# Output projection begun inside a neighbourhood attention, and two expert blocks of three strips instead of four, in one program on one Trainium2 core

## The chip, the core and the metric

One core of one Trainium2 chip runs the whole program. The number that counts is the device time of one execution in microseconds (us); before the change it was 4483.69 us, the median of 3 runs (4479.28 to 4484.81). All data are float32. The engines are TensorE (PE, its weight loads PEld), VectorE (DVE), ScalarE (ACT), GpSimd (POOL) and SyncE (SP), which issues most of the DMAs.

## What is computed

Two blocks follow each other on one sequence of 1024 tokens with 1024 channels. The first block (two layers of linear attention) is untouched. The second has two layers; layer 0 mixes the tokens by neighbourhood attention, layer 1 by grouped-query attention, and both end in a mixture of 32 experts of which each token takes 2:

```python
for i in range(DEPTH):
    h = x * (1 + sc1) + sh1
    y = neighbourhood_mixer(h, ...) if i % 2 == 0 else gqa_mixer(h, ...)   # both end in "@ w_o"
    x = layer_norm_2(ALPHA * x + (1 + g1) * y, ...)
    h = x * (1 + sc2) + sh2
    y = hierarchical_moe(h, ...)
    x = layer_norm_2(ALPHA * x + (1 + g2) * y, ...)
# neighbourhood_mixer: qkv = h @ w_qkv; o = attention(q, k, v, rpb); return o.reshape(B, S, D) @ w_o
# hierarchical_moe:    (silu(xb @ w_gate[e]) * (xb @ w_up[e])) @ w_down[e], weighted by the gates
```

## The kernel before, in words

The program is a row of stages, each a block with one hand-written instruction list per engine and semaphores between them; at a stage's end all engines meet. Four stages matter here.

**The neighbourhood attention** (`neighbourhood_stage`, layer 0) goes over 8 pairs of heads, and in each over 8 token tiles of 128: 64 steps. A step i on PE is `scores(i + 1)` (L1659), three pieces of other work, `turn(i)` (transposes, L1672), again three or four pieces, `weigh(i)` (L1689). The other work is the projection of q, k and v for the next pair (`project`, L1632 and L1641), handed out by `advance(work, n)` from a generator, one matmul (or four small ones) at a time. The last pair (steps 56 to 63) has no next pair, so its generator is empty. A step's result goes to `mixT[:, pair, tokens]`: the pair is one of the 8 channel blocks over which the output projection sums. SP loads the output weights into `xT` as soon as the last projection has read it (L1620), long before the stage ends.

**The output projection and the routing** (`out_route_stage`, both layers) computes tile by tile `mixT^T W_o` (L2301: two halves of 512 columns, 8 channel blocks each, so 16 matmuls per tile), into banks 0 and 1 of PSUM for even tiles and 2 and 3 for odd ones. DVE takes the tile (L2378 to L2401: gate, residual, layer norm, scale and shift, `h_done`), PE turns h (L2283) and multiplies by the router's weights (L2292). PE's order is: tile 0, tile 1, turn(0), tile 2, turn(1), route(0), tile 3 and so on. The rows that DVE needs (gate, layer norm, scale, shift) are loaded by SP in the first microseconds of the stage (L1361). Then DVE works out the places of the tokens (a chain of small instructions, `skip_places` among them, called twice), and SP has meanwhile loaded the weights of the first expert and half of the second.

**The experts** (`experts_stage`, both layers) run 33 blocks in the order of a table (`TURNS`). Block b below 32 holds one expert; 0 and 1 are always experts 0 and 1 (so that their weights can be loaded early), the others are taken by their number of tokens, most first. Block 32 takes what one expert has too much. A block has 4, 3 or 2 strips of 32 rows; `strips_of` gives the number: 4 for blocks 0 to 7 and 32, 3 for 8 to 19, 2 for 20 to 31. The sum is 96 strips. What doesn't fit in an expert's block goes to an overflow block; more than one of them would start a loop of further blocks behind the stage. `blocks_in_turn` writes the table so that the strips stay near three per block. For a block of S strips PE does S times 32 matmuls for gate and up (`product`, L2593), transposes (L2580, L2604) and S times 16 matmuls for down (L2616); each matmul has two records in the profile. All weights stream from HBM: 4 MB for gate and up, 2 MB for down, each with two buffers. SP issues gate and up of block n+3 when the product of block n+1 is done (`up_ready`), and down of block n+2 when down of block n is done (`y_ready`):

```python
sp.wait_ge(up_ready, n + 2); load_gate_up(n + 3)
sp.wait_ge(y_ready, n + 1);  load_down(n + 2)
sp.wait_ge(y_copied, n + 1); store_rows(...)
```

**The clearing** (`clear_overflow`, L1529) writes zeros behind the rows of every block that has fewer than 128, in the background of the first block's last output stage.

## Time and profile before

| what | value |
|---|---|
| median of 3 runs | 4483.69 us |
| the profiled execution | 4486.34 us |
| its span in the profile | 4484.4 us |
| PE busy | 4098.7 us, 91% of the span |
| DVE, ACT, POOL busy | 2013.2, 1109.2, 509.0 us |
| mean granted PE clock | 0.958 of full |
| DMA moved | 710.31 MB, mean 158 GB/s |
| neighbourhood attention | 1705 to 2238 us of the span |
| output projection and routing, layer 0 | 2238 to 2420 us |
| experts, layer 0 and layer 1 | 2420 to 3009 us and 3832 to 4418 us |

The profile page gives shares over the whole span; the change touches four stages with different limits, so each is read by itself: its busy times by window, the order in time on PE, and who ended PE's waits. "Granted clock" is the share of full PE clock (2.4 GHz) that the chip allowed; 0.50 means 1.2 GHz.

### The profile page before, as it was taken

The page shows a single profiled execution, that of the slowest core. Times are in us where ns is not written, and L with a number is a line of the kernel's source. Part 1 is how long each engine was busy: PE and PEld are TensorE (multiplying, and loading weights), DVE is VectorE, ACT ScalarE, POOL GpSimd, SP SyncE. Part 2 cuts the span into 40 slices and gives each one's busy share as a digit, 9 for nine tenths or more (in the row PEclk, how much of TensorE's full clock was granted, in tenths as well). Part 3 has the DMA queues.
Part 4 walks back from the last instruction along what each step waited for, and adds up shares of the span by engine and source line. Part 5 has one row for each costly group of instructions (what it writes and reads, how often), then busy time and mean ns, then how long its engine had stood idle before and what let it go on. Part 6 is the DMA issues. An engine that isn't in the chain of part 4 may idle for free. (4 is left out here: it accounts for less than half of the span.)

```text
span 4484.4 us, 83646 instructions
## 1 busy us (share of the span) xinstructions
PE 4098.7 (91%) x36682; PEld 2459.4 (55%) x36682; DVE 2013.2 (45%) x2980; ACT 1109.2 (25%) x1919; POOL 509.0 (11%) x348
## 2 busy tenths in 40 slices
PE   7999999899999998999896999976999998899993
PEld 3555664445556645665454556543666664555652
DVE  4565356455545554555553111106657776111114
ACT  2333223134432221222200000003444530000003
POOL 1232011032211100000000000000312200000001
PEclk9999999999999999999897999987999998899996
DMA  3323202232320244445324999982000122799996
GB/s 103 113 95 104 61 24 90 72 109 90 109 82 28 85 160 84 76 79 90 78 82 170 394 393 401 403 327 80 15 2 14 39 82 85 265 399 400 403 395 257
DMA packets 285125, 710.31 MB, mean 158 GB/s; under 512 B 57307, under 2 KB 184739, under 8 KB 267735
## 3 DMA queue, kind: packets, MB, share of 16 engines
q1 hardware_dynamic: 271751, 658.70, 42.3%
q0 software_dynamic: 11808, 41.95, 2.8%
q8 instruction: 295, 4.83, 0.4%
q10 hardware_dynamic: 1200, 4.24, 0.2%
q14 instruction: 71, 0.58, 0.0%
HBM read 631.82 MB, written 64.60 MB: 155 GB/s over the span
## 5 line engine op out<-in xcount | busy, mean ns | idle before, releaser
L493 PE MATMUL ps<-sb_xT,sb_work 128*128 128x512 f32 x768 | 359.9, 605 | 9.6 <-ACT sb_x_tok L846 5.5
L493 PE MATMUL ps<-sb_mixT,sb_work 128*128 128x512 f32 x768 | 359.5, 604 | 9.6 <-ACT sb_x_tok L846 5.5
L1632 PE MATMUL ps<-sb_xT,sb_work 128*128 128x512 f32 x512 | 236.2, 600 | 0.0
L2593 PE MATMUL ps<-sb_work,sb_mixT 128*32 128x256 f32 x3584 | 208.7, 388 | 12.4 <-DMA sb_work<-moe_w_up 11.7
L493 PEld LDWEIGHTS ps<-sb_xT,sb_work 128*128 128x128 f32 x768 | 138.0, 192 | 148.1 <-issue 130.1
L493 PEld LDWEIGHTS ps<-sb_mixT,sb_work 128*128 128x128 f32 x768 | 138.0, 192 | 147.8 <-issue 129.9
L2593 PE MATMUL ps<-sb_work,sb_xT 128*32 128x256 f32 x3584 | 204.9, 383 | 6.7 <-DMA sb_work<-moe_w_up 5.9
L2108 DVE TENSOR_REDUCE sb_cols<-ps 128x1 f32<-128x1024 f32 x128 | 150.6, 1218 | 85.8 <-PE ps L1951 85.7
L2677 DVE TENSOR_TENSOR sb_work<-ps,sb_work 128x512 f32<-128x512 f32 (+2 forms) x66 | 61.6, 933 | 260.2 <-PE ps L2616 260.2
L2660 ACT COPY sb_work<-ps 128x256 f32<-128x256 f32 (+2 forms) x66 | 31.0, 470 | 591.6 <-PE ps L2604 591.6
L2593 PEld LDWEIGHTS ps<-sb_work,sb_mixT 128*32 128x32 f32 x3584 | 117.1, 112 | 92.0 <-issue 22.7
L2593 PEld LDWEIGHTS ps<-sb_work,sb_xT 128*32 128x32 f32 x3584 | 116.0, 111 | 83.5 <-issue 14.3
L2593 PE MATMUL ps<-sb_mixT,sb_xT 128*32 128x256 f32 x2560 | 151.2, 390 | 11.0 <-DMA sb_mixT<-moe_w_up 10.0
L1927 PE MATMUL ps<-sb_work,sb_mixT 128*128 128x384 f32 x448 | 154.4, 491 | 3.2 <-PEq L93 3.2
L2593 PE MATMUL ps<-sb_xT,sb_mixT 128*32 128x256 f32 x2560 | 147.7, 383 | 8.9 <-DMA sb_xT<-moe_w_up 8.0
L2683 DVE TENSOR_TENSOR sb_work<-sb_work,ps 128x256 f32<-128x256 f32 (+2 forms) x66 | 35.8, 542 | 263.9 <-ACT sb_work L2650 263.9
L1632 PEld LDWEIGHTS ps<-sb_xT,sb_work 128*128 128x128 f32 x512 | 91.1, 190 | 104.2 <-issue 104.2
L2032 ACT ACTIVATE sb_work<-ps,sb_cols 128x1024 f32<-128x1024 f32 x128 | 142.7, 1115 | 17.9 <-DVE sb_cols L2108 12.3
L1961 PEld LDWEIGHTS ps<-sb_const,sb_work 128*128 128x128 f32 x1024 | 109.7, 141 | 63.1 <-issue 32.7
L2616 PE MATMUL ps<-sb_work 128*32 128x256 f32 x2560 | 144.1, 379 | 0.0
L1961 PE MATMUL ps<-sb_const,sb_work 128*128 128x128 f32 x1024 | 141.0, 280 | 1.9 <-DVE sb_work L2116 0.9
L1951 PE MATMUL ps<-sb_work 64*128 64x512 f32 x512 | 130.6, 629 | 6.7 <-ACT sb_work L2032 3.7
(486 smaller groups left out, 7268.4 us busy)
## 6 DMA issues: line engine op xcount, KB each, us to landing
sb_work<-moe_w_gate SPq DMA_DIRECT2D x34, 2048.0 KB, 8.2
sb_work<-moe_w_up SPq DMA_DIRECT2D x34, 2048.0 KB, 12.6
sb_work<-moe_w_down SPq DMA_DIRECT2D x32, 2048.0 KB, 21.3
sb_mixT<-moe_w_down SPq DMA_DIRECT2D x17, 2048.0 KB, 22.2
sb_xT<-moe_w_down SPq DMA_DIRECT2D x17, 2048.0 KB, 22.0
sb_xT<-moe_w_gate SPq DMA_DIRECT2D x16, 2048.0 KB, 16.0
sb_xT<-moe_w_up SPq DMA_DIRECT2D x16, 2048.0 KB, 22.1
sb_mixT<-moe_w_gate SPq DMA_DIRECT2D x16, 2048.0 KB, 15.9
```

Source lines behind the costliest of these rows:

```text
L493: last = pe.matmul(m.ps[:, bank, :], b.w[i][:, k, :], m.xT[:, k, half * HALF:(half + 1) * HALF], start=(k == 0), stop=(k == NK - 1))
L1632: last = pe.matmul(m.ps[:, bank, :], w[j // 2][:, k, :], m.xT[:, k, j % 2 * HALF:(j % 2 + 1) * HALF], start=(k == 0), stop=(k == NK - 1))
L1927: last = pe.matmul(m.ps[:, bank, 0:WIDE], m.xT[:, k, n * P:(n + 1) * P], w[:, k, :], start=(k == 0), stop=(k == NK - 1))
L1951: last = pe.matmul(m.ps[:, 2 * head + half, :], q[g % 2][j][d, t * P:(t + 1) * P], k2[g % 2][d, half * HALF:(half + 1) * HALF], start=True ...
L1961: last = pe.transpose(m.ps[:, 4 + half, b * P:(b + 1) * P], prob[i % 2][head][:, half * HALF + b * P:half * HALF + (b + 1) * P], ident(m))
L2032: act.activation(prob[i % 2][head], banks(m, 2 * head), ACT.Exp, bias=top[:, column(i, head)], accum_out=total[:, column(i, head)]).then_i ...
L2108: dve.tensor_reduce(top[:, column(i, head)], banks(m, 2 * head), AX.X, ALU.max, negate=True).then_inc(found, 1)
L2593: last = pe.matmul(strip_sums(2 + 2 * (n % 2), tile[j])[:, g, :], b.x_turned[n % 2][:, k, g * STRIP:(g + 1) * STRIP], b.gate_up[n % 2][:, ...
L2616: last = pe.matmul(strip_sums(6, tile[j])[:, g, :], b.act_turned[n % 2][:, g, tile[k]], b.down[n % 2][:, k, j * 2 * P:(j + 1) * 2 * P], st ...
L2660: act.copy(b.act_turned[n % 2][:, 0:strips[n], :], chunks(m.ps[:, 0, :])[:, 0:strips[n], :]).then_inc(h_copied, 1)
L2677: dve.tensor_tensor(b.y[n % 2][:, 0:strips[n], :], strip_sums(6)[:, 0:strips[n], :], each_chunk(b.gate_row, strips[n]), ALU.mult).then_inc ...
L2683: dve.tensor_tensor(act, act, strip_sums(2 + 2 * (n % 2))[:, 0:strips[n], P:2 * P], ALU.mult).then_inc(multiplied, 1)
```

## The change

Three things are edited.

1. In the last pair of the neighbourhood attention, from its fourth tile (step 59) on, PE gets pieces to do: the output projection of three half tiles, over the 7 channel blocks that are finished then. `OUT_BEGUN` names (tile, half, bank): (0, 0, 6), (0, 1, 7), (1, 0, 2), so 21 matmuls. Two pieces stand before `turn` and three after it. Ahead of the first PE waits for the output weights. The output stage of layer 0 then computes only the eighth channel block of these three half tiles; tile 0 lies in banks 6 and 7 there, not 0 and 1. Layer 1 gets `begun=()` and stays as it was.
2. Blocks 0 and 1 have 3 strips instead of 4, in both layers: 94 strips. The table of turns is made anew with that start. Counted with the reference's own routing on its inputs, experts 0 and 1 get 81 and 55 tokens in layer 0, and 54 and 68 in layer 1; three strips hold 96.
3. `skip_places` has one more DVE instruction (it must know the narrower first blocks), and the clearing writes two more places of 32 rows.

```diff
-    places = [(b, rows_of(b)) for b in range(WIDE_BLOCKS, N_EXPERTS)] + [(b, 0) for b in range(N_FIXED, N_BLOCKS)]
+    places = [(b, rows_of(b)) for b in range(N_EXPERTS) if rows_of(b) < P] + [(b, 0) for b in range(N_FIXED, N_BLOCKS)]
...
+OUT_BEGUN = ((0, 0, 6), (0, 1, 7), (1, 0, 2))
...
+            def begin_out():
+
+                pe.wait_ge(out_loaded, 16 * (NK // 2))
+                for t, half, bank in OUT_BEGUN:
+                    for k in range(pairs - 1):
+                        pe.matmul(m.ps[:, bank, :], m.mixT[:, k, t * P:(t + 1) * P], m.xT[:, k, half * HALF:(half + 1) * HALF],
+                                  start=(k == 0), stop=False)
+                        yield
...
-                    work = project(pair + 1) if pair + 1 < pairs else iter(())
+                    work = project(pair + 1) if pair + 1 < pairs else begin_out()
                 if i + 1 < count:
                     scores(i + 1)
-                advance(work, 3)
+                if pair + 1 < pairs or t >= 3:
+                    advance(work, 3 if pair + 1 < pairs else 2)
                 turn(i)
-                advance(work, 3 if t < NT - 1 else 4)
+                if pair + 1 < pairs or t >= 3:
+                    advance(work, 3 if t < NT - 1 else 4)
                 weigh(i)
...
-    return 4 - (block >= WIDE_BLOCKS) - (block >= MIDDLE_BLOCKS) if block < N_EXPERTS else 4
+    if block >= N_EXPERTS:
+        return 4
+    return 4 - (block < N_FIRST) - (block >= WIDE_BLOCKS) - (block >= MIDDLE_BLOCKS)
...
-    order, strips = list(range(N_FIRST)), 4 * N_FIRST
+    order, strips = list(range(N_FIRST)), 3 * N_FIRST
...
+    def y_bank(t):
+        return 6 if t == 0 and begun else 2 * (t % 2)
...
-                    for k in range(NK):
-                        last = pe.matmul(m.ps[:, 2 * (t % 2) + half, :], m.mixT[:, k, t * P:(t + 1) * P],
+                    for k in range(NK - 1 if (t, half, y_bank(t) + half) in begun else 0, NK):
+                        last = pe.matmul(m.ps[:, y_bank(t) + half, :], m.mixT[:, k, t * P:(t + 1) * P],
...
-                do(dve.tensor_scalar(spare, at, MIDDLE_BLOCKS - 0.5, None, ALU.is_gt))
+                do(dve.tensor_scalar(spare, at, N_FIRST - 0.5, None, ALU.is_lt))
+                do(dve.scalar_tensor_tensor(spare, at, MIDDLE_BLOCKS - 0.5, spare, ALU.is_gt, ALU.add))
```

How the instructions stand now at the places that matter. PE from the scores of step 63 to the second tile of layer 0's output projection (L1659 scores, L1672 turn, L1689 weigh, L2301 projection, L2283 turning h), before:

```order
L1659 MATMUL ps<-sb_work 128x384 x2
L1672 MATMUL ps<-sb_const,sb_work 128x128 x6
L1689 MATMUL ps<-sb_work 64x128 x6
L1672 MATMUL ps<-sb_const,sb_work 128x128 x6
L1689 MATMUL ps<-sb_work 64x128 x6
L1573 UNCONDITIONAL_BRANCH
L2275 UNCONDITIONAL_BRANCH
L2301 MATMUL ps<-sb_xT,sb_mixT 128x512 x32
L2283 MATMUL ps<-sb_const,sb_work 128x128 x8
L2301 MATMUL ps<-sb_xT,sb_mixT 128x512 x16
```

The same place with the change (L1661, L1674, L1691, L2320 and L2302 are the same lines moved down, L1700 the new pieces):

```order
L1661 MATMUL ps<-sb_work 128x384 x2
L1700 MATMUL ps<-sb_xT,sb_mixT 128x512 x2
L1674 MATMUL ps<-sb_const,sb_work 128x128 x6
L1700 MATMUL ps<-sb_xT,sb_mixT 128x512 x3
L1691 MATMUL ps<-sb_work 64x128 x6
L1700 MATMUL ps<-sb_xT,sb_mixT 128x512
L1674 MATMUL ps<-sb_const,sb_work 128x128 x6
L1691 MATMUL ps<-sb_work 64x128 x6
L1575 UNCONDITIONAL_BRANCH
L2294 UNCONDITIONAL_BRANCH
L2320 MATMUL ps<-sb_xT,sb_mixT 128x512 x11
L2302 MATMUL ps<-sb_const,sb_work 128x128 x8
```

Steps 59 to 62 have five new matmuls each, step 63 has one, and the first two tiles of the output stage have 11 matmuls left of 32.

PE in the first blocks of the experts, before:

```order
L2593 MATMUL ps<-sb_work,sb_mixT 32x256 x128
L2580 MATMUL ps<-sb_const,sb_mixT 128x128 x8
L2593 MATMUL ps<-sb_xT,sb_mixT 32x256 x32
L2604 MATMUL ps<-sb_const,sb_work 128x128 x4
L2593 MATMUL ps<-sb_xT,sb_mixT 32x256 x32
L2580 MATMUL ps<-sb_const,sb_mixT 128x64 x8
L2593 MATMUL ps<-sb_xT,sb_mixT 32x256 x64
L2616 MATMUL ps<-sb_mixT,sb_work 32x256 x64
```

With the change (L2613, L2600, L2624, L2636 are the same lines moved down):

```order
L2613 MATMUL ps<-sb_work,sb_mixT 32x256 x96
L2600 MATMUL ps<-sb_const,sb_mixT 128x96 x8
L2613 MATMUL ps<-sb_xT,sb_mixT 32x256 x32
L2624 MATMUL ps<-sb_const,sb_work 128x128 x3
L2613 MATMUL ps<-sb_xT,sb_mixT 32x256 x32
L2600 MATMUL ps<-sb_const,sb_mixT 128x96 x8
L2613 MATMUL ps<-sb_xT,sb_mixT 32x256 x32
L2636 MATMUL ps<-sb_mixT,sb_work 32x256 x48
```

The products of blocks 0 and 1 have 96 matmuls each instead of 128. The strips by turn were 4, 4, 2, 2, twelve times 3, then six times (4, 2), then 4, 2, 2, 2, 2; now they are fourteen times 3, then six times (4, 2), then 4 and six times 2. So the stage ends with six narrow blocks in place of four.

## Rows read from the trace of the kernel before

**Rows 1.** Windows of the last pair; columns: us, busy (x count) by engine, PEclk, DMA
```profile
2188.00:2238.00 50.00, 28.70 (x172) 17.69 (x172) 27.21 (x77) 12.15 (x36) 0.00 (x0) 0.73 0.21 85
2200.00:2204.00 4.00, 4.00 (x22) 2.44 (x18) 1.34 (x5) 0.57 (x2) 0.00 (x0) 0.50 0.02 5
...
2238.00:2242.00 4.00, 3.79 (x5) 1.65 (x6) 0.67 (x7) 1.28 (x1) 0.13 (x1) 0.57 0.68 240
```

**Rows 2.** Timeline of PE: start, us, line, shapes, count, idle time before
```profile
2172.55 0.92 PE L1659 MATMUL ps<-sb_work 64*128 64x384 f32 x4
...
2180.23 0.92 PE L1659 MATMUL ps<-sb_work 64*128 64x384 f32 x4
...
2210.22 1.65 PE L1659 MATMUL ps<-sb_work 64*128 64x384 f32 x4
...
2233.45 0.88 PE L1689 MATMUL ps<-sb_work 128*64 128x128 f32 x12 [1.71 <-ACT sb_work L1745]
...
2238.21 29.40 PE L2301 MATMUL ps<-sb_xT,sb_mixT 128*128 128x512 f32 x64 [1.50 <-PEq L93]
2267.45 1.04 PE L2283 MATMUL ps<-sb_const,sb_work 128*128 128x128 f32 x8
2268.32 13.90 PE L2301 MATMUL ps<-sb_xT,sb_mixT 128*128 128x512 f32 x32
```

**Rows 3.** Timeline of DVE in layer 0's output projection, first tile
```profile
2241.76 0.69 DVE L2366 TENSOR_SCALAR sb_work<-sb_work 128x1024 f32<-128x1024 f32 x1 [3.04 <-DMA sb_work<-scratch_mods]
2253.99 1.23 DVE L2378 TENSOR_TENSOR sb_work<-ps,sb_work 128x1024 f32<-128x1024 f32 x1 [11.53 <-PE ps L2301]
...
2258.07 1.28 DVE L2391 SCALAR_TENSOR_TENSOR sb_x_tok<-sb_x_tok,sb_moments,sb_work 128x1024 f32<-128x1024 f32 x1
...
2261.97 1.22 DVE L2401 TENSOR_TENSOR sb_work<-sb_work 128x1024 f32<-128x1024 f32 x1
```

**Rows 4.** Timeline of SP, the last row loads; then landing times of line L1361
```profile
2239.51 1.22 SPq L1361 DMA_DIRECT2D sb_work<-scratch_mods  x2
...
DMA to landing us min/median/max: 3.4/6.1/9.3
```

**Rows 5.** Timeline of DVE, start of `skip_places`
```profile
2394.00 0.18 DVE L2457 TENSOR_SCALAR sb_work<-sb_work 128x32 f32<-128x32 f32 x1
2394.22 0.19 DVE L2458 SCALAR_TENSOR_TENSOR sb_work<-sb_work 128x32 f32<-128x32 f32 x1
```

**Rows 6.** SP's own waits in the stage with the clearing: total, times, longest
```profile
SPq L1384 <- PEq L1384: 28.9, 1, 28.9
```

**Rows 7.** Windows of the experts of layer 0, same columns as rows 1
```profile
2457.00:2700.00 243.00, 234.08 (x3981) 141.44 (x3973) 28.12 (x41) 18.68 (x40) 11.79 (x13) 0.99 1.02 393
...
2900.00:2950.00 50.00, 47.47 (x798) 28.51 (x794) 5.52 (x8) 3.98 (x8) 1.79 (x2) 0.97 0.98 379
```

**Rows 8.** Timeline of SP: gate of the third and of the fourth block
```profile
2439.42 0.40 SPq L2724 DMA_DIRECT2D sb_work<-moe_w_gate  x1
...
2457.08 0.34 SPq L2724 DMA_DIRECT2D sb_xT<-moe_w_gate  x1
```

**Rows 9.** Timeline of PE in the experts: two unhindered middle blocks
```profile
2529.39 3.64 PE L2593 MATMUL ps<-sb_work,sb_mixT 128*32 128x256 f32 x64
...
2541.56 5.36 PE L2616 MATMUL ps<-sb_work 128*32 128x256 f32 x96
2546.74 3.64 PE L2593 MATMUL ps<-sb_xT,sb_mixT 128*32 128x256 f32 x64
```

**Rows 10.** Timeline of PE: blocks that waited for gate and up
```profile
2510.32 5.35 PE L2593 MATMUL ps<-sb_xT,sb_mixT 128*32 128x256 f32 x64 [3.84 <-DMA sb_xT<-moe_w_up]
...
2656.53 3.66 PE L2593 MATMUL ps<-sb_xT,sb_mixT 128*32 128x256 f32 x64 [2.31 <-DMA sb_xT<-moe_w_up]
...
2923.36 5.35 PE L2593 MATMUL ps<-sb_work,sb_mixT 128*32 128x256 f32 x64 [2.53 <-DMA sb_work<-moe_w_up]
...
2990.88 6.26 PE L2593 MATMUL ps<-sb_work,sb_mixT 128*32 128x256 f32 x64 [4.93 <-DMA sb_work<-moe_w_up]
```

More of the change, by code:

```diff
@@ L1550, in neighbourhood_stage @@
     bias_loaded, moved, masked = (s["loaded_d"], s["loaded_e"]), s["prefetched"], s["signal_0"]
+    out_loaded = s["stored"]
     (projected, evicted, scored, biased, exponent, inverted, normalised, turned_a, turned_b, copied_a, copied_b,
@@ L1617, in _ @@
                     load_weights(2, pair + 1)
-            load_out_weights(sp, m, a["na_w_o_2"][0], s["stored"])
-            sp.wait_ge(s["stored"], 16 * (NK // 2))
+            load_out_weights(sp, m, a["na_w_o_2"][0], out_loaded)
+            sp.wait_ge(out_loaded, 16 * (NK // 2))
         @block.tensor
@@ L2200, with out_route_stage @@
 TURNS = blocks_in_turn()
-def out_route_stage(nc, m, l, a, ln_g, ln_b, gate, modulate, x_affine=None):
+def out_route_stage(nc, m, l, a, ln_g, ln_b, gate, modulate, x_affine=None, begun=()):
     s = m.sem
@@ L2377, in _ @@
                 dve.wait_ge(y_ready, t + 1)
-                dve.tensor_tensor(y[t % 2], banks(m, 2 * (t % 2)), gate_row, ALU.mult).then_inc(y_gated, 1)
+                dve.tensor_tensor(y[t % 2], banks(m, y_bank(t)), gate_row, ALU.mult).then_inc(y_gated, 1)
                 dve.wait_ge(y_gated, t + 1)
@@ L3009, in program @@
         x_affine = (a["ln_g_2"][l - 1, 1], a["ln_b_2"][l - 1, 1]) if l else None
-        out_route_stage(nc, m, l, a, a["ln_g_2"][l, 0], a["ln_b_2"][l, 0], mods[l][2], mods[l][3:5], x_affine)
+        out_route_stage(nc, m, l, a, a["ln_g_2"][l, 0], a["ln_b_2"][l, 0], mods[l][2], mods[l][3:5], x_affine,
+                        begun=OUT_BEGUN if l % 2 == 0 else ())
         ln_rows = a["ln_g_2"][l, 1], a["ln_b_2"][l, 1]
```

## The prediction

> **What bounds the kernel now.** I read the windows first, then PE's timeline, then the waits, each for the stages that the change touches. In the last pair of the neighbourhood attention PE is busy 28.70 of 50 us [rows 1]: the pair has no projection to mix in, so each step is a chain from scores over DVE and ScalarE to the weighted sum. PE stands between the links, and the granted clock falls to 0.50, which is 1.2 GHz, even while PE is busy all of 4 us. The same 4 us show a DMA share of 0.02: the output weights, which SP fetches before, have landed by about 2200, ten microseconds before the first new matmul may ask for them at 2210.22. In the output projection PE has no gap (64 records in 29.40 us, then 32 in 13.90 us) and DVE waits 11.53 us for it [rows 2, 3]: PE bounds it. In the experts both PE and the DMA engines are full: DMA share 1.02 at 393 GB/s over 243 us [rows 7]. Who ends the waits decides it. From turn 5 (2510.32) to turn 32 (2990.88) PE began a block every 17.80 us, and waited for gate and up at both ends and between [rows 10]; an unhindered block of three strips takes PE 2546.74 - 2529.39 = 17.35 us [rows 9]. So the stream of weights sets the pace, by a narrow margin.
>
> **The change part by part.** All steps are against the profiled execution (4486.34 us, which is 2.65 us above the median of the runs).
>
> *The moved matmuls, where they go.* A 128x512 matmul takes PE 13.90 / 16 = 0.87 us at full clock [rows 2]. A step of a full pair, with six of them, takes 2180.23 - 2172.55 = 7.68 us [rows 2]; with five it is 7.68 - 0.87 = 6.8. That is longer than the chain of a last-pair step at full clock, so PE sets the step. Step 59's part begins with the scores at 2210.22 at the low clock (1.65 us against 0.92) [rows 2]. PE then has work without a gap, and at 2238 the full clock came back within about 4 us (0.57 over the first 4), at a price of 29.40 - 2 x 13.90 = 1.6 us [rows 1, 2]. I take that price once: step 59 is 6.8 + 1.6 = 8.4, three further steps are 20.4, so the sum of step 62 (`weigh`) ends at 2239.0 and begins at 2238.2 instead of 2233.45. Step 63 has one matmul, 0.87. The stage ends **5.6 us later** (4.8 + 0.87). Bounds: 3 us, if the clock is back sooner and the old idle time of 1.7 us before each `weigh` hides a part; 10 us, if it is back a step and a half later.
>
> *Where they come from.* The first two tiles keep 11 of 32 matmuls: 11 x 0.87 = 9.6 us. But turn(0) needs DVE's first tile. From the stage's start s = 2238.21, DVE's gate row is ready at s + 4.2 (2241.76 + 0.69) [rows 3]. From there the part up to the moments takes 2258.07 - 2253.99 = 4.1 us, to s + 8.3 [rows 3]. Then DVE needs the scale and shift rows: the last are issued from 2239.51 for 1.22 us and land up to 9.3 us later, about 2249.7, s + 11.4 [rows 4]. The remaining part takes 2261.97 + 1.22 - 2258.07 = 5.1, so h is done at s + 16.5. Before, turn(0) began at 2267.45 = s + 29.2 [rows 2]. The gain is **12.7 us**, not the 18.3 of 21 matmuls: PE is out of work at s + 9.6 and stands some 7 us for the row loads. That is a new wait, and turn(0) and tile 2 are queued behind it. It is long enough for the clock: after the last pair's gaps the row shows 0.50 [rows 1], so I charge the 1.6 us again. From tile 2 on PE is the bound again, since DVE needs about 10 us per tile and PE 16. The Trainium skill (TensorE: Matmul & The Clock Gate, the section on the HAM clock gate) says that the throttled clock is the default and only sustained activity lifts it; by that rule the new gap costs the clock, as charged; with a clock that ignored gaps the sum would be 1.6 us better. Net of this part: 5.6 - 12.7 + 1.6 = **-5.5 us**. Bounds -9 and 0.
>
> *The experts.* A strip costs PE 3.6 us in the product and 5.36 / 3 = 1.8 in down [rows 9]. Two strips fewer would be 10.8 us of PE, but PE is not the pace. What the edit does to the stream: SP issued gate and up of turn 2 at 2439.42 when product 0 was done, and of turn 3 at 2457.08 when product 1 was done [rows 8]. Between, 4 MB at 393 GB/s [rows 7] take 10.7 of 17.7 us, so the engines ran dry; only from the second issue on is the stream whole. That issue now comes after two products of three strips, 2 x 3.6 = 7.2 us earlier. Thereafter the same 30 pairs of matrices go through. The strips save 128 KB each in the two stores and one gather behind that point, 0.39 MB or 1.0 us. The stream stays whole: a block moves 6.3 MB of weights and 0.8 MB of tokens and results, 7.1 MB or 18 us at 393 GB/s, and the fourteen blocks of three strips ask for the next load every 17.35 us. The wide blocks may leave a hole, as now (0.98 in one window [rows 7]); I take off 0.7. The end is unchanged: the last block has two strips in both. So **-7.5 us per layer**, -15.0 for both (the second runs the same program). Bounds per layer: -8.5, and -1 (rival B).
>
> *Small edits.* `skip_places` has one instruction more, called twice per layer, on DVE's chain to the experts: 2394.22 - 2394.00 = 0.22 us [rows 5], four times, **+0.9 us**. The two added clearing writes of 128 KB each cost nothing: SP stood 28.9 us at the end of that stage waiting for PE alone [rows 6]; without this cover they would cost under 2 us.
>
> Sum: -5.5 - 15.0 + 0.9 = **-19.6 us**: 4466.7 against the profiled execution, 4464.1 against the median.
>
> **The rivals.**
>
> B, *PE is the pace of the experts and the narrow tail eats the gain.* For it: between the waits of rows 10 most blocks ran without one, and 17.35 is only 3% below 17.80. Then the shorter products save 10.8 us of PE, but the stage now ends in six narrow blocks instead of four. PE needs 17.35 - 5.4 = 12.0 us for one, the stream (2990.88 - 2923.36) / 4 = 16.9 [rows 10], so two more blocks wait 4.9 each: -10.8 + 9.8 = -1.0 per layer. Total -5.5 + 0.9 - 2.0 = -6.6: 4477.1. Against it: PE waited 4.93 us for the last block and the DMA share is 1.02. The Trainium skill (DMA: Bandwidth & Descriptors, "Where 436 GB/s comes from") gives the fabric 435 GB/s and HBM 358 per core; at the first a block of 7.1 MB would take 16.3 us, below PE's 17.35, and B would hold; the trace has 393 and 379 [rows 7], between the two, and decides against it. Chance 0.15.
>
> C, *the low clock stays* (the slower side). If the full clock isn't granted from step 59 to the end of tile 2, a step takes 2 x 2.4 for its own work and 5 x 1.74: 13.5 us. Four steps and step 63 end the stage 31 us later; the first two tiles take 19.1 instead of waiting until 16.5, so the gain falls to 10.1; tile 2 costs 13.9 more. 31 - 10.1 + 13.9 + 0.9 - 15 = +20.7: 4504.4. Each us of low clock costs half a us, so it decides from some 60 us of low clock on. For it: 0.50 with PE fully busy [rows 1]. Against: at 2238 it was gone after a few us of gapless work [rows 2]. Chance 0.04.
>
> D, *the projection gives nothing*: the stage ends 10 us later (the clock comes back late) and the output stage gains 10 to 11. Total -14: 4469.7. Chance 0.10.
>
> E, *the change doesn't do what it says*: experts 0 or 1 have over 96 tokens, a second overflow block starts the loop behind the stage. One more block of 6.3 MB at 393 GB/s with nothing beside it, 16 us, then some 23 of PE for four strips: +39 per layer, 4503 or more. The counts in the description (at most 81) exclude it but for a slip. Chance 0.01.
>
> **How the numbers follow.** A measurement of this kernel can tell about 0.2%, 9.0 us. My forecast has 0.70, its own range is 4457 to 4471. It and D lie beyond 9 us; of B a third does, if the tail eats less. Faster 0.70 + 0.10 + 0.05 = 0.85; within 0.2%: 0.10 of B and 0.01 of C, 0.11; slower 0.03 + 0.01 = 0.04. The range for 8 in 10 runs from 4456 (both bounds on the good side) to 4477 (B).
>
> **What would show it.** Right: from step 59 on a step of about 6.8 us at clock 1.00; an idle time of 6 to 7 us on PE before the first turn of h, with DVE's first tile ending 16 to 17 us after the stage's start; gate and up of turn 3 issued some 7 us earlier after the stage's start; waits for gate and up of about 5 us at most of the last five turns; an experts stage shorter by 7 to 8 us in both layers. Wrong: the experts' stage shorter by 1 to 3 us with DMA share under 1.00 in the middle (B); clock 0.50 beyond the first two new matmuls (C, D); a gap on PE of under 3 us in the output stage, which would say that the rows land earlier than I take them to and that more than 12.7 us is gained.

## The result and the profile after

| | before | after |
|---|---|---|
| median, runs of one call | 4481.48 us (4 runs, 4474.98 to 4484.81) | 4454.57 us (4 runs, 4447.35 to 4456.38) |
| ratio, 95% interval | | 0.9934 [0.9922, 0.9946] |
| the profiled execution, its span | 4486.34, 4484.4 us | 4455.61, 4453.7 us |
| PE busy, records | 4098.7 us | 4066.9 us, x36294 (388 fewer) |
| DMA moved | 710.31 MB | 709.73 MB |

Forecast was 4464.1 in a range of 4456 to 4477. The kernel became 27 us faster instead of 19.6, and its median lies 1.4 us below the range's low end. Between the two profiled executions the difference is 30.7 us:

| stretch | before | after | difference | forecast |
|---|---|---|---|---|
| start of the attention | 1709.09 | 1707.83 | -1.3 | not touched |
| attention, to the start of the output stage | 529.12 | 535.27 | +6.15 | +5.6 |
| from there to the first turn of h | 29.24 | 17.00 | -12.24 | -12.7 |
| first to second turn of h | 14.60 | 16.81 | +2.21 | +1.6 |
| second turn of h to the first expert product | 140.51 | 140.59 | +0.1 | +0.45 |
| experts, layer 0 (first product to last matmul's end) | 586.51 | 574.49 | -12.0 | -7.5 |
| experts, layer 1 | 583.26 | 570.83 | -12.4 | -7.5 |
| between and behind the experts | 892.07 | 890.88 | -1.2 | +0.45 |

The forecast column has the prediction's term for each stretch. The attention and the output stage came out 1.6 us worse than forecast in sum (-3.9 against -5.5), the experts gained 9.4 us more. The 1.3 us ahead of the attention lie within the scatter: its start lies between 1706.0 and 1709.7 us in all the traces here. PE around the new matmuls, timeline of after (columns as in [rows 2]):

```profile
2208.98 1.65 PE L1661 MATMUL ps<-sb_work 64*128 64x384 f32 x4
2210.56 3.33 PE L1700 MATMUL ps<-sb_xT,sb_mixT 128*128 128x512 f32 x4
...
2217.86 0.92 PE L1661 MATMUL ps<-sb_work 64*128 64x384 f32 x4
...
2224.65 0.92 PE L1661 MATMUL ps<-sb_work 64*128 64x384 f32 x4
...
2243.10 9.68 PE L2320 MATMUL ps<-sb_xT,sb_mixT 128*128 128x512 f32 x22 [1.50 <-PEq L93]
2260.10 1.97 PE L2302 MATMUL ps<-sb_const,sb_work 128*128 128x128 f32 x8 [7.32 <-DVE sb_work L2420]
2261.86 15.21 PE L2320 MATMUL ps<-sb_xT,sb_mixT 128*128 128x512 f32 x32
2276.91 1.04 PE L2302 MATMUL ps<-sb_const,sb_work 128*128 128x128 f32 x8
```

Step 59 takes 2217.86 - 2208.98 = 8.88 us (forecast 8.4), the next 6.79 (6.8). Then the new wait: PE stands 7.32 us ahead of the first turn of h, and behind it the low clock, 1.97 us for a turn that takes 1.04 and 15.21 for a tile that takes 13.90 [rows 2]. That is 0.93 + 1.31 = 2.2 us. What PE waited for stands on DVE, first tile (timeline of after; [rows 3] before):

```profile
2246.62 0.69 DVE L2385 TENSOR_SCALAR sb_work<-sb_work 128x1024 f32<-128x1024 f32 x1 [3.00 <-DMA sb_work<-scratch_mods]
...
2251.19 0.21 DVE L2405 BATCH_NORM_AGGREGATE sb_moments<-sb_stats 128x2 f32<-128x12 f32 x1
2254.92 1.28 DVE L2410 SCALAR_TENSOR_TENSOR sb_x_tok<-sb_x_tok,sb_moments,sb_work 128x1024 f32<-128x1024 f32 x1 [3.52 <-DMA sb_work<-scratch_mods]
...
2258.82 1.22 DVE L2420 TENSOR_TENSOR sb_work<-sb_work 128x1024 f32<-128x1024 f32 x1
```

DVE waits twice, for the gate row and for scale and shift, which land 11.8 us after the stage's start at 2243.10 (forecast 11.4). PE no longer holds DVE: the 11.53 us of [rows 3] are gone.

In the experts, SP's issues of the third and fourth block's gate (after; [rows 8] before):

```profile
2431.10 0.40 SPq L2744 DMA_DIRECT2D sb_work<-moe_w_gate  x1
...
2444.88 0.34 SPq L2744 DMA_DIRECT2D sb_xT<-moe_w_gate  x1
```

From the first product (2417.50, before 2422.56) to the second of these issues it is 27.38 us, before 34.52: 7.1 us earlier, in layer 1 7.5. Forecast was 7.2. PE in that stage (timeline of after; [rows 9, 10] before):

```profile
2466.69 3.64 PE L2613 MATMUL ps<-sb_xT,sb_mixT 128*32 128x256 f32 x64
...
2484.04 3.64 PE L2613 MATMUL ps<-sb_work,sb_mixT 128*32 128x256 f32 x64
...
2501.39 3.64 PE L2613 MATMUL ps<-sb_xT,sb_mixT 128*32 128x256 f32 x64
...
2623.45 3.66 PE L2613 MATMUL ps<-sb_work,sb_mixT 128*32 128x256 f32 x64 [0.40 <-DMA sb_work<-moe_w_up]
...
2925.77 5.77 PE L2613 MATMUL ps<-sb_xT,sb_mixT 128*32 128x256 f32 x64 [6.06 <-DMA sb_xT<-moe_w_up]
...
2943.74 5.32 PE L2613 MATMUL ps<-sb_work,sb_mixT 128*32 128x256 f32 x64 [3.63 <-DMA sb_work<-moe_w_up]
...
2959.54 3.66 PE L2613 MATMUL ps<-sb_xT,sb_mixT 128*32 128x256 f32 x64 [1.90 <-DMA sb_xT<-moe_w_up]
...
2975.01 5.05 PE L2613 MATMUL ps<-sb_work,sb_mixT 128*32 128x256 f32 x64 [3.24 <-DMA sb_work<-moe_w_up]
```

Blocks follow each other every 17.35 us, and in layer 0 the first wait for weights comes 206 us after the first product (0.40 us at 2623.45). Before, turn 5 waited 3.84 us, 88 us after the first product [rows 10]. The sum of these waits in layer 0 hardly changed, 19.7 to 19.0 us; most of it now stands in the tail, behind the wide blocks.

The part that was not forecast is the stream. I call stream the time from the issue of the fourth block's gate to the first matmul that uses the last block's up: 533.80 and 532.71 us before (layers 0 and 1), 530.13 and 527.50 after, so 3.7 and 5.2 us shorter, where the forecast had 0.3. Windows of 60 us, the first and the third behind that issue (columns: us, busy (x count) of PE, PEld, DVE, ACT, POOL, PEclk, DMA share, GB/s), after:

```profile
2444.88:2504.88 60.00, 59.98 (x1045) 36.06 (x1037) 7.54 (x11) 4.36 (x9) 2.72 (x3) 1.00 1.02 396
2564.88:2624.88 60.00, 59.60 (x1041) 35.79 (x1036) 7.72 (x11) 4.85 (x10) 2.77 (x3) 1.00 1.02 399
```

and before:

```profile
2457.08:2517.08 60.00, 56.16 (x939) 33.65 (x935) 7.36 (x11) 4.21 (x10) 2.71 (x3) 0.97 1.00 381
2577.08:2637.08 60.00, 57.24 (x992) 34.41 (x985) 7.52 (x11) 4.34 (x9) 2.71 (x3) 1.00 1.02 384
```

Between the two lies one window of 402 GB/s in both. In the 180 us the new kernel moves (15 + 0 + 15) GB/s x 60 us = 1.8 MB more, which is 4.5 us of stream. From then on the rates agree: 399 GB/s to the end of the stream, 400 before. A part of the first window belongs to the start and not to what follows: its DMA share is 1.00 before and 1.02 after, and over all complete kernels with loads asked for as in these two it is 0.98 to 1.00 where blocks 0 and 1 have four strips, 1.02 where they have three.

### The profile page after: what moved, and what is told of

The parts are those of the page before. It is cut to its first block and busy times, and to the rows that moved or that the text cites. A ratio compares the mean times of both kernels' runs of the same rounds, so it can differ in the third digit from the quotient of the medians.

```text
span 4453.7 us, 82876 instructions
## 1 busy us (share of the span) xinstructions
PE 4066.9 (91%) x36294; PEld 2439.0 (55%) x36294; DVE 2011.5 (45%) x2984; ACT 1109.3 (25%) x1919; POOL 509.4 (11%) x348
## 2 busy tenths in 40 slices
DMA packets 284642, 709.73 MB, mean 159 GB/s; under 512 B 57339, under 2 KB 184259, under 8 KB 267255
## 5 line engine op out<-in xcount | busy, mean ns | idle before, releaser
L2613 PE MATMUL ps<-sb_work,sb_mixT 128*32 128x256 f32 x3520 | 204.3, 387 | 10.7 <-DMA sb_work<-moe_w_up 10.0
L2613 PE MATMUL ps<-sb_work,sb_xT 128*32 128x256 f32 x3520 | 202.7, 385 | 8.8 <-DMA sb_work<-moe_w_up 8.1
L2680 ACT COPY sb_work<-ps 128x384 f32<-128x384 f32 (+2 forms) x66 | 30.6, 464 | 581.3 <-PE ps L2624 581.3
L2697 DVE TENSOR_TENSOR sb_work<-ps,sb_work 128x768 f32<-128x768 f32 (+2 forms) x66 | 60.6, 918 | 254.2 <-PE ps L2636 254.2
L2613 PEld LDWEIGHTS ps<-sb_work,sb_mixT 128*32 128x32 f32 x3520 | 114.4, 112 | 88.5 <-issue 21.0
L2613 PEld LDWEIGHTS ps<-sb_work,sb_xT 128*32 128x32 f32 x3520 | 114.0, 111 | 85.1 <-issue 17.2
L2613 PE MATMUL ps<-sb_xT,sb_mixT 128*32 128x256 f32 x2496 | 144.6, 384 | 9.6 <-DMA sb_xT<-moe_w_up 9.0
L2613 PE MATMUL ps<-sb_mixT,sb_xT 128*32 128x256 f32 x2496 | 145.6, 386 | 8.4 <-DMA sb_mixT<-moe_w_up 7.8
L2703 DVE TENSOR_TENSOR sb_work<-sb_work,ps 128x384 f32<-128x384 f32 (+2 forms) x66 | 35.3, 535 | 247.1 <-ACT sb_work L2670 247.1
L2636 PE MATMUL ps<-sb_work 128*32 128x256 f32 x2496 | 140.6, 379 | 0.0
L1741 ACT ACTIVATE sb_work<-sb_work,sb_cols 128x384 f32<-128x384 f32 x128 | 77.6, 607 | 238.2 <-DVE sb_cols L1786 238.2
```

What stands on the lines that cost most here:

```text
L1741: act.activation(p, p, ACT.Exp, bias=top[:, column(i, head)], scale=-1.0, accum_out=total[:, column(i, head)]).then_inc(exponent, 1)
L2613: last = pe.matmul(strip_sums(2 + 2 * (n % 2), tile[j])[:, g, :], b.x_turned[n % 2][:, k, g * STRIP:(g + 1) * STRIP], b.gate_up[n % 2][:, ...
L2636: last = pe.matmul(strip_sums(6, tile[j])[:, g, :], b.act_turned[n % 2][:, g, tile[k]], b.down[n % 2][:, k, j * 2 * P:(j + 1) * 2 * P], st ...
L2680: act.copy(b.act_turned[n % 2][:, 0:strips[n], :], chunks(m.ps[:, 0, :])[:, 0:strips[n], :]).then_inc(h_copied, 1)
L2697: dve.tensor_tensor(b.y[n % 2][:, 0:strips[n], :], strip_sums(6)[:, 0:strips[n], :], each_chunk(b.gate_row, strips[n]), ALU.mult).then_inc ...
L2703: dve.tensor_tensor(act, act, strip_sums(2 + 2 * (n % 2))[:, 0:strips[n], P:2 * P], ALU.mult).then_inc(multiplied, 1)
```

## The experiments

### Splitting the change

What was to be told apart: how much each half gives, and whether the surplus in the experts comes from the two narrower blocks (an earlier issue) or from the new order of the turns.

**Projection alone:** the change, with blocks, order and `skip_places` of before.

```diff
-    return 4 - (block < N_FIRST) - (block >= WIDE_BLOCKS) - (block >= MIDDLE_BLOCKS)
+    return 4 - (block >= WIDE_BLOCKS) - (block >= MIDDLE_BLOCKS)
...
-    order, strips = list(range(N_FIRST)), 3 * N_FIRST
+    order, strips = list(range(N_FIRST)), 4 * N_FIRST
```

> Only the begun output projection; the experts as in the kernel before. My forecast of this part was -5.5 us; the trace of the change reads 4.9 us later at the end of the attention, 12.2 us gained up to the first turn of h, 2.2 us lost to the low clock behind the gap: -5.1 in sum. If the traces tell the truth: 4 to 6 us faster than before. If the extra gain of the whole change lies in this part (a second effect of the fillers): 10 us or more faster.

Measured: 4481.77 us against 4482.77, ratio 0.9996 [0.9987, 1.0005], 11 runs. By the time alone no gain can be told; the interval reaches from -5.8 to +2.2 us. Its trace shows the stretches of after to a tenth of a microsecond: attention 535.31, first turn of h at 16.96, from the attention's start to the first expert product 709.66 us against 709.67 after and 713.47 before. So this half gives 3.8 us. That stretch repeats well: it is 713.5 to 713.7 us in the four traces without the moved matmuls and 709.3 to 709.7 in the eight with all 21 of them. The expert stages, which the edit leaves as before, hide it in the total: in this trace they are 588.3 and 584.6 us against 586.5 and 583.3, together 3.2 us longer.

**Experts alone:** `begun=()`, no pieces in the last pair.

```diff
-                    work = project(pair + 1) if pair + 1 < pairs else begin_out()
+                    work = project(pair + 1) if pair + 1 < pairs else iter(())
```

> Only the two narrower first blocks with the new order of turns and the longer skip_places; no projection begun. My forecast of this part was -15.0 + 0.9 = -14.1 us. The two traces read -12.0 and -12.4 us for the two experts stages. If that is real and not a difference between two single executions: 23 us faster than before. If it is scatter: 14 us.

Measured: 4458.16 us, ratio 0.9945 [0.9932, 0.9959], -24.6 us. The forecast of this half was -14.1, or -23 if the traces of the stages were right. Nearly the whole gain is the experts'. The two halves add up: -1.0 and -24.6 give -25.6, the change measured -26.9.

**Strips alone:** as "experts alone", with the order of turns of before.

```diff
-TURNS = blocks_in_turn()
+TURNS = [0, 1, 20, 21, 8, 9, 10, 11, 12, 13, 14, 15, 16, 17, 18, 19, 32, 22, 2, 23, 3, 24, 4, 25, 5, 26, 6, 27, 7, 28, 29, 30, 31]
```

> As e2, but the turns in the order of before: strips 3, 3, 2, 2, twelve times 3 and so on, four narrow blocks at the end. Theory S (the stream of weights sets the pace all through; only its start matters): the start is 7.2 us earlier as in e2, so the same time as e2. Theory P (PE's own work sets the pace in most of the stage and the order decides how much of it is lost in waits): slower than e2 by 4 us or more in both layers together, because turns 2 and 3 are narrow, PE runs ahead early and waits at turn 5 as in the kernel before (3.8 and 4.1 us).

Measured: 4462.79 us, ratio 0.9953 [0.9939, 0.9967], -20.0 us. The fourth block's gate is issued 7.5 and 8.3 us earlier, the streams are 534.1 and 531.5 us, as before. Its stages end 576.8 and 575.4 us after the first product. The early waits are back, 60 and 79 us behind the first product (PE, timeline of this kernel):

```profile
2482.05 3.66 PE L2611 MATMUL ps<-sb_work,sb_mixT 128*32 128x256 f32 x64 [2.36 <-DMA sb_work<-moe_w_up]
...
2501.62 4.93 PE L2611 MATMUL ps<-sb_xT,sb_mixT 128*32 128x256 f32 x64 [3.85 <-DMA sb_xT<-moe_w_up]
```

Against "experts alone" the old order costs 4.6 us (4462.79 against 4458.16, the fastest execution of the one just behind the slowest of the other). But the -20.0 are 5.9 us more than the forecast of -14.1, which had no term for the order; against the trace of before its two stages are only some 17.5 us shorter. Where the rest comes from is open.

**Order alone:** before, with the planner started at six strips, so the new order stands with blocks 0 and 1 still of four.

```diff
-    order, strips = list(range(N_FIRST)), 4 * N_FIRST
+    order, strips = list(range(N_FIRST)), 3 * N_FIRST
```

> The kernel before with only the order of turns of the change: blocks 0 and 1 keep 4 strips, then twelve times 3, and six narrow blocks at the end. Theory S: no issue of the stream moves, 0 +- 2 us against before. Theory P: the early wait at turn 5 goes, 4 to 8 us faster in both layers together, unless the longer narrow tail takes it back.

Measured: 4475.86 us, ratio 0.9983 [0.9974, 0.9992], -6.9 us, 11 runs. No early waits: the first stands 392 us behind the first product. Streams 532.3 and 529.9 us. The first and the third window of its stream:

```profile
2454.87:2514.87 60.00, 60.00 (x1050) 36.11 (x1046) 7.35 (x10) 4.45 (x9) 2.72 (x3) 1.00 0.99 372
2574.87:2634.87 60.00, 60.00 (x1039) 36.23 (x1042) 7.32 (x11) 5.31 (x11) 3.66 (x4) 1.00 1.02 402
```

and the third of "strips alone":

```profile
2569.37:2629.37 60.00, 56.20 (x965) 34.04 (x955) 6.87 (x10) 4.34 (x9) 2.74 (x3) 1.00 1.02 381
```

So both edits gain: the strips by the earlier issue, the order by a shorter stream. The order's part is what the forecast left out.

### Is it PE or the stream?

**Less PE:** from the third turn on the products sum over 5 of 8 channel slices; the loads stay.

```diff
-            for k in range(NK):
+            for k in (range(NK) if n < 2 or n_blocks == 1 else (*range(NK // 2), NK - 1)):
```

> The change, but the products of all turns from the third on sum over 5 of their 8 slices of channels (3 are left out), so PE has about 4 us less per block and the stream alone sets the pace. Only layer 0 is read, since the wrong values route layer 1 otherwise. The stream is the time from the issue of turn 3's gate to the first matmul of turn 32; in the change 530.1 us, with the old order 533 to 537. Theory S (the stream is whole and its rate is the chip's): 528 to 532 as before, with PE waiting in nearly every turn. Theory P (PE's work held the stream back): 520 or less, rate above 405 GB/s. Theory L (the stream runs slower when PE is behind it and waits, as in the old order between 120 and 180 us after turn 3's issue, 384 GB/s against 399 to 406): 535 or more, at 390 GB/s.

Its values differ from then on, so layer 1 routes its tokens otherwise, and layer 0 is the one to read. Measured once: 4460.82 us. The stages end 575.5 and 575.1 us after the first product (after: 574.5, 570.8), the streams are 533.4 and 532.6. PE is busy for 77 us less in the stream of layer 0 (434.6 against 511.1, though at a mean clock of 0.91 instead of 0.99) and the stage is no shorter. The stream lies between what the expectation gave to S (528 to 532) and to L (535 or more), so neither is met. Totals of PE's waits (us in total, times, longest) in layer 0, this kernel:

```profile
PE ps L2613 <- DMA sb_work<-moe_w_up: 52.3, 15, 6.6
PE ps L2613 <- DMA sb_xT<-moe_w_up: 46.5, 14, 6.4
```

and after:

```profile
PE ps L2613 <- DMA sb_work<-moe_w_up: 10.0, 5, 3.6
PE ps L2613 <- DMA sb_xT<-moe_w_up: 9.0, 3, 6.1
```

What PE saves comes back as waits: 98.8 us against 19.0. Rival B had PE as the pace, and falls here. The surprise is in the windows (same columns; the first, third and fifth behind the issue of the fourth block's gate):

```profile
2446.75:2506.75 60.00, 54.01 (x844) 31.18 (x840) 7.53 (x11) 4.83 (x10) 2.71 (x3) 0.91 1.02 384
2566.75:2626.75 60.00, 45.82 (x717) 26.46 (x709) 6.32 (x10) 4.34 (x9) 2.76 (x3) 0.94 1.02 389
...
2686.75:2746.75 60.00, 50.85 (x776) 29.36 (x772) 6.91 (x10) 4.92 (x11) 3.69 (x4) 0.91 1.02 412
```

At the same DMA share of 1.02 the engines move 384 to 389 GB/s where PE waits from the start, against 396 to 402 where it doesn't. Yet in the fifth window it is 412, and PE still waits there: it does so at 29 of the 33 blocks of this stage. And the first window of "order alone" has 372 GB/s at a share of 0.99 with a PE that never waits. So whether PE waits does not decide the rate by itself. The Trainium skill (DMA: Bandwidth & Descriptors, "Where 436 GB/s comes from") gives 358 GB/s for HBM per core; this stream is above it in every window of before, after and "less PE", so no ceiling at that figure is seen here.

**Less PE, old order:** the same edit with the table of "strips alone".

> As e9, with the turns in the order of before and blocks 0 and 1 of three strips. Theories S, P and L: the same stream as e9 within 2 us, because the order mattered only through PE. If the order itself sets the rate of the stream (which sizes of stores and gathers stand beside which loads), it is again 3 to 5 us longer than e9.

Measured once: 4461.93 us, streams 534.2 and 535.0, 384 GB/s over the first 180 us of the stream (387 in "less PE"). With PE out of the way the two orders lie 0.8 us apart in layer 0, the layer to read, and 2.4 in layer 1. Single executions with one and the same order differ by up to 4.0 us in layer 0 (528.3 to 532.3), so this fits an order that works through the time at which PE is done with its blocks, but it does not show it: an effect of a few us on the transfers themselves would not be seen in one run each.

**Half of down:** the reverse, half of each down matrix not loaded from the third turn on.

```diff
-                sp.dma_start(b.down[n % 2], source(n, "down").rearrange("(k p) n -> p k n", p=P)).then_inc(loads[n % 2][1], 16)
+                k = slice(0, QUARTERS) if n < 2 else slice(0, QUARTERS // 2)
+                sp.dma_start(b.down[n % 2][:, k, :], source(n, "down").rearrange("(k p) n -> p k n", p=P)[:, k, :]).then_inc(
+                    loads[n % 2][1], 16)
```

> The change, but from the third turn on only the first half of each down matrix is loaded (1 MB less per block, 6.0 instead of 7.05 MB), PE's work as it was. Only layer 0 is read. PE is then the pace: no waits for gate and up, and the stage lasts as long as PE's own work, that is its 570.8 us less the 18.9 us of waits and about 4 us of low clock behind them: 547 to 549 us. If it stays above 555, something other than the bytes of the stream (the issue behind up_ready, the latency) makes PE wait.

Measured once: 4422.75 us; both stages end 555.0 and 555.1 us after the first product. I had expected 547 to 549, but counted from the 570.8 us at which the last group of matmuls in after begins, not ends; counted so, this stage takes 551.4 us. What is left of the miss, 2 to 4 us, is about the 4 us of low clock that I had taken off. The window over the stream of layer 0 (same columns):

```profile
2445.52:2957.42 511.90, 507.73 (x8700) 305.23 (x8692) 61.25 (x92) 41.16 (x90) 25.60 (x28) 1.00 0.91 352
```

PE is busy nearly without a break and waits 4.2 us in all for weights. So PE alone sets about 555 us, and after, at 574.5 and 570.8, is 16 to 20 us above it. Less work for PE gained nothing ("less PE"), 1 MB less per block gained all of those 16 to 20 us.

**Middle reversed:** blocks 8 to 19 in reverse; strips by turn unchanged.

```diff
-TURNS = blocks_in_turn()
+TURNS = [0, 1] + list(range(19, 7, -1)) + [32, 20, 2, 21, 3, 22, 4, 23, 5, 24, 6, 25, 7, 26, 27, 28, 29, 30, 31]
```

> The change with the twelve middle blocks (8 to 19) in reversed order: the same strips by turn, but other experts at each turn. If the rate of the stream hangs on which weights are read when, the time moves by 3 us or more; if it hangs on the pattern of strips, it is the same as the change within 2 us (27 to 28 us faster than before).

Measured: 4452.2 us, ratio 0.9932 [0.992, 0.9945] (the change: 0.9934), streams 531.7 and 525.7, within the spread of the new order. Which expert's weights are read when makes no difference that can be told here.

### Why the stream is slower beside a waiting PE

The idea was that a PE that takes each block at once lets SP ask for the next loads while the others are under way, and that too many transfers in the queues lower the rate. **Less PE, later issue** takes the gate and up of block n+3 behind the down of n+2:

```diff
-                if n + 3 < N_FIXED:
-                    sp.wait_ge(up_ready, n + 2)
-                    load_gate_up(n + 3)
                 sp.wait_ge(y_ready, n + 1)
                 if n + 2 < N_FIXED:
                     load_down(n + 2)
+                if n + 3 < N_FIXED:
+                    sp.wait_ge(up_ready, n + 2)
+                    load_gate_up(n + 3)
```

> e9 with one edit more: SP issues gate and up of turn n+3 only after the down product of turn n (behind the down load of turn n+2) and not already when the product of turn n+1 is done; fewer bytes are outstanding. Theory Q (many outstanding transfers lower the rate): in the first 180 us after turn 3's issue 396 GB/s or more instead of 384 to 389, and a stream of 530 us or less in spite of the later issue, unless the queue runs dry (DMA share under 1.00). Rival (the rate there hangs on something else): again 384 to 389 GB/s, 533 us or more. Layer 0 is read.

Measured once: 4525.89 us, the stage ends 608.1 us after the first product, 379 GB/s over the 558 us of the stream at a share of 0.98. Its first three windows have 376, 375 and 392 GB/s at shares of 0.98, 0.98 and 1.01. The queues ran dry now and then, which the expectation had excluded, so this run decides neither way: no higher rate was seen, but queues that are less full and never dry were not tried.

**Later issue:** the same swap on the full change.

> The change with the same later issue. PE works 17.35 us per block of three strips and a load now has 5 to 6 us less to land, 17 us instead of 23: with 16 us for gate and 22 for up from issue to landing PE waits in most turns. Both theories: slower than the change by 2 to 10 us; if it is faster, fewer outstanding transfers are a gain in themselves.

Measured: 4643.83 us (4 runs), ratio 1.0365 [1.0348, 1.0382]. That is 163 us slower than before and 190 slower than after, where I had expected 2 to 10. Window over most of layer 0's stream:

```profile
2450.29:3011.80 561.51, 490.75 (x7973) 291.04 (x7966) 55.53 (x81) 38.00 (x81) 24.63 (x27) 0.94 0.87 341
```

The DMA share is 0.87 where after has 1.01 over its stream, and PE waits 4 to 6 us for every second block, in layer 0 85 us in all, at a mean clock of 0.94. From the first product to the start of the last group of matmuls layer 0 takes 663.1 us against 570.8 in after: the issue directly behind the product is worth some 90 us per layer. With two buffers, a load asked for one down later is asked for too late. The same swap costs 33 us where PE has less to do (608.1 against 575.5), so here, unlike in after, PE's own time counts. Why "less PE" runs at the lower rate in its first 180 us stays open.

### Making the moved matmuls cheaper

The change puts 21 matmuls where steps then take 6.8 us and takes them from a place that then waits 7.3 us for DMAs. Two ways out.

**Two halves:** tile 0 only.

```diff
-OUT_BEGUN = ((0, 0, 6), (0, 1, 7), (1, 0, 2))
+OUT_BEGUN = ((0, 0, 6), (0, 1, 7))
```

> The whole change, but only the two half tiles of tile 0 begun (14 matmuls, still two ahead of turn and three behind it). Theory G (the third half tile is moved for nothing, since PE stands 7.3 us for DVE's first tile in the output stage): the attention ends 2.7 us later than in the kernel before instead of 6.1, the first turn of h still starts 17.0 us after the stage's start, the idle time ahead of it shrinks to about 1.2 us and the 2.2 us of low clock behind it go: 5 to 6 us faster than the change. Rival (every matmul moved into the attention is a gain): 4 to 6 us slower than the change.

Measured: 4446.63 us, ratio 0.9923 [0.9909, 0.9936]. The stage of the attention is 531.65 us, the first turn of h comes at 16.62 with a gap of 0.93 instead of 7.32. From the attention's start to the first expert product: 703.4 us, 6.3 less than after (expected 5 to 6).

**Two halves, spread:** also none ahead of `turn`, three behind it in each step.

```diff
-                if pair + 1 < pairs or t >= 3:
-                    advance(work, 3 if pair + 1 < pairs else 2)
+                if pair + 1 < pairs:
+                    advance(work, 3)
```

> As e5, but the 14 matmuls only between turn and weigh, three per step in steps 59 to 62 and two in step 63. Theory G: a step is then about 5.1 us, at full clock, less than the 6.3 us of the empty steps at the low clock; the attention ends at the same time as in the kernel before or 1 to 2 us sooner: 8 to 9 us faster than the change. If the clock stays at 0.50 with only three matmuls per step, a step takes 9 us or more and it is slower than e5.

Measured: 4442.65 us, ratio 0.9917 [0.9903, 0.993]. PE, timeline of this kernel:

```profile
2212.09 3.45 PE L1700 MATMUL ps<-sb_xT,sb_mixT 128*128 128x512 f32 x6
...
2216.28 0.92 PE L1661 MATMUL ps<-sb_work 64*128 64x384 f32 x4
...
2221.32 0.92 PE L1661 MATMUL ps<-sb_work 64*128 64x384 f32 x4
...
2236.30 15.69 PE L2320 MATMUL ps<-sb_xT,sb_mixT 128*128 128x512 f32 x36 [1.51 <-PEq L93]
2252.68 1.09 PE L2302 MATMUL ps<-sb_const,sb_work 128*128 128x128 f32 x8 [0.70 <-DVE sb_work L2420]
```

A step is 2221.32 - 2216.28 = 5.04 us. Before, with nothing in it, a step took 2216.52 - 2210.22 = 6.30 us [rows 2], at the low clock. The scores of its next step, from the trace of before:

```profile
2216.52 1.65 PE L1659 MATMUL ps<-sb_work 64*128 64x384 f32 x4
```

They take 1.65 us there and 0.92 here. The whole stage takes 528.35 us, less than before the change (529.12), with 14 matmuls more in it. They stand where PE waited 1.70 us for ScalarE's part of the softmax, and the clock stays full behind them. From the attention's start to the first product it is 699.9 us, 9.8 less than after (expected 8 to 9).

**Rows early:** the full change, with the gate and the two layer norm rows loaded in the attention stage, behind the output weights; layer 0's output stage leaves those loads and their waits out.

```diff
             load_out_weights(sp, m, a["na_w_o_2"][0], out_loaded)
+            rows = [m.work[:, n * SEQ:(n + 1) * SEQ] for n in range(3)]
+            load_rows(sp, [(rows[2], m.mods[0, 2 * D:3 * D]), (rows[0], a["ln_g_2"][0, 0]), (rows[1], a["ln_b_2"][0, 0])],
+                      rows_early)
```

> The whole change, and SP loads the gate and the two layer norm rows of layer 0 already in the attention, behind the output weights; only scale and shift are loaded in the output stage. If the row loads are what DVE's first tile waits for: the first turn of h starts about 11 us after the stage's start instead of 17.0, PE's idle time there falls from 7.3 to about 1.5 us: 6 to 8 us faster than the change. If it is DVE's own work that sets it: no difference.

Measured: 4444.61 us, ratio 0.9915 [0.9901, 0.9928]. The first turn of h (this kernel's timeline):

```profile
2241.46 9.68 PE L2325 MATMUL ps<-sb_xT,sb_mixT 128*128 128x512 f32 x22 [1.50 <-PEq L93]
2252.79 1.09 PE L2307 MATMUL ps<-sb_const,sb_work 128*128 128x128 f32 x8 [1.65 <-DVE sb_work L2427]
2253.72 13.90 PE L2325 MATMUL ps<-sb_xT,sb_mixT 128*128 128x512 f32 x32
```

It comes 2252.79 - 2241.46 = 11.33 us after the stage's start, 5.7 earlier than in after; the gap is 1.65, and the clock stays at full (13.90 for the next tile, not 15.21). That the row loads made most of the gap is shown by this; the 1.65 us that are left are spent on DVE's own instructions. The path to the first product is 701.9 us, 7.8 less than after (expected 6 to 8).

**Both:** two halves spread, and the rows early.

> e6 and the early rows of e7 together. PE has 18 matmuls left in the first two tiles, 15.7 us, and DVE's first tile is done after 11 us, so PE is the bound again: 1 to 2 us faster than e6, 10 us faster than the change.

Measured: 4439.87 us (4434.64 to 4447.0), ratio 0.9912 [0.9898, 0.9925]. PE, the end of the first projection:

```profile
2235.34 15.69 PE L2325 MATMUL ps<-sb_xT,sb_mixT 128*128 128x512 f32 x36 [1.51 <-PEq L93]
2250.87 1.04 PE L2307 MATMUL ps<-sb_const,sb_work 128*128 128x128 f32 x8
```

No gap is left, 699.0 us to the first expert product, 10.7 less than after. This is the lowest median of the complete kernels, below before and below after (slowest execution 4447.0 us, fastest of after 4447.35). Against "two halves, spread" the times can't be told apart; on the path the early rows add 0.9 us, so they are worth little once PE has its 18 matmuls back.

## Why the prediction was right, and where it failed

**The moved matmuls.** Attention +5.6: measured +6.15, 0.5 of it in step 59 (8.88 against 8.4). Gain up to the first turn of h -12.7: -12.24. The gap of some 7 us: 7.32. The landing of scale and shift at s + 11.4: 11.8. DVE's first tile ended 16.9 us after the stage's start, forecast 16 to 17. That DMA rows, not PE, would bound the start of the stage is shown by "rows early", which took 5.7 us from it. The low clock behind the gap +1.6: 2.2. Net -5.5: measured -3.9 (by the total of "projection alone" -1.0, in an interval of -5.8 to +2.2). That 21 matmuls there were too many was in these numbers, and I did not draw it: 9.6 us of work ahead of a first tile that is ready at 16.5 leaves room for seven more of them.

**Small edits.** `skip_places` +0.45 per layer: the stretch that holds it and the shorter turn of the first block came out at +0.1. The clearing was taken at nothing, and nothing was seen of it.

**The experts' start.** "That issue now comes after two products of three strips, 2 x 3.6 = 7.2 us earlier": 7.1 and 7.5. "So the engines ran dry" is stronger than the trace: between the two issues the share was 0.81 before, and is 0.93 after. The term was right all the same.

**The step that failed:** "Thereafter the same 30 pairs of matrices go through", with only 1.0 us for the saved bytes and 0.7 back for holes, at a rate taken as fixed, and with no term for the order of the turns. The stream became 3.7 and 5.2 us shorter, against 0.3 forecast. The pairs are the same, but the rate is not a constant of the stream: over its first 180 us it is 389 GB/s before and 399 after. With the new order (fourteen turns of three strips ahead of the wide blocks, none of two) PE needs 17.35 us per block, and in layer 0 of after the weights are there in time for the first 206 us. Before, two narrow blocks stood third and fourth; PE went through them faster than their successors' weights came, and waited at turn 5. Counted over all complete kernels with the early issue, the streams of the old order are 533.8 to 536.7 us in layer 0 and 531.5 to 534.0 in layer 1 (three kernels), those of the new one 528.3 to 532.3 and 525.7 to 529.9 (eight kernels). They don't overlap in either layer, and the means are 4.6 and 4.9 us apart. By the time of the program the order is worth 6.9 us with wide first blocks ("order alone") and 4.6 with narrower ones ("strips alone" against "experts alone").

The sum of the three parts then reads: moved matmuls -5.5 forecast, -1.0 measured by the total and -3.8 by the trace; strips -14.1 forecast, -20.0 measured; order 0 forecast, -4.6 measured; together -25.6, where the whole change measured -26.9. So the order accounts for 4.6 of the 7.3 us that the forecast missed. The surplus of the strips is not explained, and its size is loose: the interval of "strips alone" goes from -27.3 to -14.8 us. The remaining 1.2 us in layer 0 are the time behind the last landing, 17.0 against 18.2, where the last block's first group took 5.05 us instead of 6.26 [rows 10]; layer 1 has none of it.

Why the order changes the rate stays open. Early waits and a lower rate often stand together: the first 180 us have 384 to 393 GB/s in before, "projection alone", "strips alone", "less PE" and "less PE, old order", and 394 to 403 where PE hardly waits early ("half of down" aside, which asks for less). But a cause is not shown by that, and two rows speak against the simple one, that a waiting PE lowers the rate: 372 GB/s without any wait, and 412 with a PE that waits.

**The rivals.** B falls: PE does less and nothing gets shorter. Its picture of the tail was right all the same, waits of 6.06, 3.63, 1.90 and 3.24 us stand there; but the stream beneath them did not become longer, so no cost of their own is seen. C's low clock was gone within step 59. D (a gain of 10 to 11 and a stage 10 later) did not come. The range was too narrow on its good side because I bounded the experts at -8.5 per layer, from the issue and the bytes alone, where -12.0 and -12.4 were measured; the rate of [rows 7] was a mean of one long window, and windows of 60 us of the same trace go from 381 to 405 GB/s.

## What to carry to other kernels

When a stream of weights and an engine are within a few per cent of each other, try the order of the blocks: here one that never let the engine run ahead of the loads early on made each stream some 4 to 5 us shorter. Read the stream's rate in several windows before it is taken as a constant, and give the order a term of its own in the forecast. Work moved into an engine's waits costs nothing only where it fits the wait: 14 matmuls behind the turn shortened the stage, 21 spread over both places lengthened it by 6 us and left a hole of 7 us where they came from. Before work is taken ahead of a first result, look at which DMA that result needs next.

## What was not expected of the hardware

The DMA engines' busy share says little of the rate: at 1.02 they moved 378 to 413 GB/s in windows of 60 us of the same kind of load. SP's time for an issue is no constant either: the same four stores took it 7.52 us in "less PE" and 1.93 at the same place in after.

The timeline of SP in "less PE":

```profile
2517.03 7.52 SPq L2571 DMA_DIRECT2D scratch_y<-sb_work  x4
```

and in after, there and later:

```profile
2520.16 1.93 SPq L2571 DMA_DIRECT2D scratch_y<-sb_work  x4
...
2836.89 8.16 SPq L2571 DMA_DIRECT2D scratch_y<-sb_work  x4
```

This does not go with the rate: the last row stands in a window of 400 GB/s, and in "less PE, later issue", at 379 GB/s, where the loads are asked for later and fewer are under way, the four stores took 1.8 to 2.6 us all through the stream of layer 0.

Idle gaps on PE of 0.70 and 1.65 us left the full clock in place, one of 7.32 us did not, and its price was 2.2 us on top of the gap. Three matmuls of 0.87 us per step, put into a wait, made the step itself 1.3 us shorter: with the clock at full, the scores, turn and weighted sum of a step took 0.92, 0.87 and 0.88 us instead of 1.65, 1.54 and 1.55.
